# Which units read x's first two chunks from stepped copies, and where the copies are made, in a three-block transformer kernel on one core

## The chip, the core and the metric

The kernel runs on one core of one Trainium2 chip. The metric is the device time of one execution in microseconds. Times inside an execution are counted from the start of its span, the time between its first and its last instruction. TensorE is called PE, VectorE DVE, ScalarE ACT and GpSimd POOL in the rows of the profile.

## What is computed

For x of 256 tokens by 1024 features the kernel runs three blocks in turn, each a mixing layer and a feed-forward part:

```python
x = x + gla_layer_mix(rmsnorm(x, g_mix[0]), mem_k, mem_v, ...)   # block A: gated linear attention + memory attention
x = x + conv_ffn(rmsnorm(x, g_ffn[0]), w_up[0], ...)             # f0
shared = nsa_shared_kv(x, g_kv, w_kv, ...)                       # kv
x = x + nsa_layer_mix(rmsnorm(x, g_mix[1]), shared, ...)         # block B: sparse attention + memory attention
x = x + conv_ffn(rmsnorm(x, g_ffn[1]), w_up[1], ...)             # f1
x = rmsnorm(x, g_final)
h = concat([meta, x]); h = h + mix(rmsnorm(h, norm1_w))          # block C: forgetting attention + pooling
out = h + (silu(n2 @ w_gate) * (n2 @ w_up)) @ w_down             # f2, n2 = rmsnorm(h, norm2_w)
```

All of it is float32. Nearly all the work is in the products of normalized activations and weights.

## The kernel before

**Units.** The weights are cut into 146 units of 128 x 2048 columns, named in the order in which they are used (`Aq`, `Ak`, `Am0`, ..., `f0u0`, `f0u1`, ..., `f0d10`, `kvc`, `kvk`, `Bq0`, ...). SyncE loads a unit into one of three slots of `raw`; ScalarE casts it to a high part `wh` in the fp32r format, VectorE subtracts to get the low part `wl` (line 1279). Activations are split in the same way, in eight chunks of 128 features by 256 tokens: ScalarE writes the high part of a chunk with its gain, VectorE the low part (`enter`, line 1287), and `x_lo` counts the chunks entered. A product is then three matmuls: high by high, low by high and high by low (`mm3`), all issued at line 417. The division by the norm is done later, on the products.

**Forms of a unit on PE.** `unit_f` (line 435) and `part_f` (line 456, a range of chunks) keep a block of 128 columns of weights stationary and move a chunk of x through: for each chunk two blocks of three matmuls, so 48 matmuls for a unit and 6 for a chunk. `unit_t` (line 491) has x stationary and moves the weights, for two tiles of 128 tokens: 3 matmuls for a chunk and tile, so 48 for a unit as well. Each waits for the unit's low weights (`w_low`) and for each chunk (`ready(c)`). Every engine runs its own program in the order written, so that what stands behind a wait waits too.

**Where the operands lie.** Each chunk of x lies in `xh` and `xl` at a pitch of 320 columns, and its 256 tokens begin at column 48 modulo 64 of the partition, for every chunk. The memory and the attention's outputs lie in `coh` and `col` with the chunk offsets

```python
CO = [0, 256, 512, 768, 1568, 1840, 1024, 1280]
```

so that all chunks begin at 48 modulo 64 but chunk 4, at 16, and chunk 5, at 32. Weights begin at 0 modulo 64 (at 32 for the units of `unit_t`, at 48 for `Ck` and `Cu`).

**The copies.** `xkh` and `xkl` hold copies of chunks 0 and 1 of x at a pitch of 272 columns, so that they begin at 16 and at 32. POOL makes them (`first_two`, line 2532: four copies of 128x256, lines 2536 and 2537) once the low part of chunk 1 is there, and counts them in `x_two`. They are made for A, f0, f1, C and f2. They are called stepped copies here. With the argument `two`, `unit_f` reads chunks 0 and 1 from them, after a wait on `x_two`. Before the change these units do so: `Am1`; u2, u3 and u5 of each feed-forward part (`ffn`, line 633); u12 of f1; and `Cq1`.

**The order around the change.** u2 and u3 stand behind short breaks in the run of large matmuls: `sums` (four products of one column, for the variances) and `norm_spread` (two transposes). `Am0`'s first half stands behind `sums`, `Bq0` behind `norm_spread`, `m0k0` behind the products of `tri`, `Av0` and `Av1` behind small products of the memory attention, and the halves of `Bm0` and `Bm1` behind small products of the sparse and the memory attention. u5 stands behind `down(tag, 0)`, 48 large matmuls, and u12 of f1 behind the sums of the meta tokens. POOL also computes the powers for the norms (`power`, line 2527), in its program's order: ..., first_two f0, power f0, power B, two memsets, first_two f1, ...

Of the kernel before, what the change touches and what calls it, by code (L numbers as in the profile page):

```python
# [142 lines left out]
ENTER = {n: 8 * i for i, n in enumerate(["A", "mem0", "mem1", "f0", "kv", "B", "f1"])}  # L143
ENTER.update(meta=56, C=57, f2=65)
NORM = {n: i for i, n in enumerate(["A", "mem", "f0", "B", "f1", "f2"])}
TWO = {n: i for i, n in enumerate(["A", "f0", "f1", "C", "f2"])}
POW = {n: i for i, n in enumerate(["A", "mem", "gla", "f0", "B", "f1", "meta", "C1", "C2", "q", "k", "f2"])}

SQ = {"A": 0, "mem": 8, "f0": 16, "B": 24, "f1": 32, "meta": 40, "f2": 41}
RES = {"f0": 0, "f1": 4, "f2": 8}  # L150
POOLED = [0, 2, 5, 9]
MIX = {"f0": 0, "f1": 1, "f2": 2}
KORD = [0, 1, 2, 3, 4, 5, 6, 7]
KOUT = [4, 5, 6, 7, 0, 1, 2, 3]
NR = NH = 3
# [12 lines left out]
def program(nc, ctx, w_d, x_d, mem_d, meta_d, small_d, const_d, gmask_d, nsac_d, sel_d, out_d):  # L168
# [246 lines left out]
    def pe_program(pe, t):  # L415
# [16 lines left out]
            m = src.shape[0]  # L432
            return pe.transpose(out, src, cn("ident")[0:m, 0:m])  # L433

        def unit_f(name, bank, a_h, a_l, ready, two=None):


            i = U[name]
            H, L = v3(wslot(wh, i), 256), v3(wslot(wl, i), 256)
            P = ps.open(name, bank)  # L440
            t.wait_ge(*ps.vacant(name))
            for c in range(8):
                t.wait_ge(*w_low(i, c // 4))
                t.wait_ge(*ready(c))
                if two and c < 2:
                    t.wait_ge(*x_two.at(TWO[two]))
                    x_h, x_l = XKH(c), XKL(c)
                else:
                    x_h, x_l = a_h(c), a_l(c)
                for j in range(2):  # L450
                    o = slice(j * 128, (j + 1) * 128)
                    last = mm3(P[:, j * 256:j * 256 + T], H[:, c, o], L[:, c, o], x_h, x_l, c == 0 and j == 0, c == 7)
            last.then_inc(*ps.full(name))
            used[i] = ps.ready(name)

        def part_f(name, bank, chunks, ready, a_h=XH, a_l=XL):

            i = U[name]
            H, L = v3(wslot(wh, i), 256), v3(wslot(wl, i), 256)
            if chunks[0] == 0:  # L460
                ps.open(name, bank)
                t.wait_ge(*ps.vacant(name))
            P = ps[name]
            for c in chunks:
                t.wait_ge(*(w_lo0.at(QUART.index((i, c // 2))) if i < 2 else w_low(i, c // 4)))
                t.wait_ge(*ready(c))
                for j in range(2):
                    o = slice(j * 128, (j + 1) * 128)
                    last = mm3(P[:, j * 256:(j + 1) * 256], H[:, c, o], L[:, c, o], a_h(c), a_l(c), c == 0 and j == 0, c == 7)
            if chunks[-1] == 7:  # L470
                last.then_inc(*ps.full(name))
                used[i] = ps.ready(name)
# [15 lines left out]
            if 1 in blocks:  # L488
                used[i] = ps.ready(f"{name}.1")

        def unit_t(name, bank, a_h, a_l, ready, tiles=(0, 128), turn=(0, 1)):

            i = U[name]
            H, L = v3(wslot(wh, i), 256), v3(wslot(wl, i), 256)
            for n, a in enumerate(tiles):
                if n not in turn:
                    continue
                at = f"{name}.{n // 2}"
                if n % 2 == 0:
                    ps.open(at, bank())  # L500
                    t.wait_ge(*ps.vacant(at))
                O = ps[at][:, (n % 2) * 256:(n % 2) * 256 + 256]
                for c in range(8):
                    t.wait_ge(*w_low(i, c // 4))
                    t.wait_ge(*ready(c))
                    mm(O, a_h(c)[:, a:a + 128], H[:, c, :], c == 0, False)
                    mm(O, a_l(c)[:, a:a + 128], H[:, c, :], False, False)
                    last = mm(O, a_h(c)[:, a:a + 128], L[:, c, :], False, c == 7)
                if n % 2 == 1:
                    last.then_inc(*ps.full(at))  # L510
            if len(tiles) - 1 in turn:
                used[i] = ps.ready(at)
# [120 lines left out]
        def ffn(tag):  # L633
            x_in = entered(tag)
            unit_f(f"{tag}u0", bank_a(), XH, XL, x_in)
            unit_f(f"{tag}u1", bank_a(), XH, XL, x_in)
            sums(tag, bank_b())
            unit_f(f"{tag}u2", bank_a(), XH, XL, x_in, tag)
            norm_spread(tag, bank_b(), rst_)
            unit_f(f"{tag}u3", bank_a(), XH, XL, x_in, tag)  # L640
            unit_f(f"{tag}u4", bank_a(), XH, XL, x_in)
            down(tag, 0)
            unit_f(f"{tag}u5", bank_a(), XH, XL, x_in, tag)
            down(tag, 1)
            for p in range(2, 10):
                unit_f(f"{tag}u{2 * p + 2}", bank_a(), XH, XL, x_in, tag if tag == "f1" and p == 5 else None)
                unit_f(f"{tag}u{2 * p + 3}", bank_a(), XH, XL, x_in)
                down(tag, p)
                if tag == "f1" and p == 4:
                    meta_sums()  # L650
            down(tag, 10)
# [12 lines left out]
        quarters(P, T, lambda c: wn[:, c, :], lambda c: xs[c], True, True).then_inc(*ps.full("alr"))  # L664
        t.wait_ge(*d_cst.at(0))
        sums("A", bank_b())
        part_f("Am0", bank_a(), range(0, 4), x_a)
        norm_spread("A", bank_b(), rst_)
        part_f("Am0", None, range(4, 8), x_a)

# [71 lines left out]
        last.then_inc(*ps.full("tri"))  # L742
        m_0, m_1 = entered("mem0"), entered("mem1")
        qA = lambda h: f"Am{h // 2}"
        unit_f("m0k0", bank_a(), CH, CL, m_0)
        unit_f("m0k1", bank_a(), CH, CL, m_0)
        level(0)
        sums("mem", bank_b())
# [20 lines left out]
        mem_scores(0, 3, bank_b(), mqA, qA)  # L769
        mem_turn(0, 1, bank_b())  # L770
        mem_out(0, 0, bank_b())
        unit_t("Av0", bank_a, XH, XL, x_a)
        mem_turn(0, 2, bank_b())
        mem_out(0, 1, bank_b())
        unit_t("Av1", bank_a, XH, XL, x_a)
        mem_turn(0, 3, bank_b())
        mem_out(0, 2, bank_b())
        summed(0)
# [150 lines left out]
        sums("B", 4)  # L929
        part_f("kvk", 1, range(4, 8), kv_in, CH, CL)  # L930
        norm_spread("B", 5, rst_)
        unit_f("Bq0", 3, XH, XL, x_b)
        P = ps.open("gates", 0)
        t.wait_ge(*ps.vacant("gates"))
        t.wait_ge(*s_wn.at(1))
# [19 lines left out]
        squeeze(1, 0, 2)  # L955
        nsa_scores(2)
        squeeze(1, 1)
        part_f("Bm0", 1, range(0, 4), x_b)
        nsa_scores(3)
        P = ps.open("gT", 0)  # L960
        t.wait_ge(*ps.vacant("gT"))
# [20 lines left out]
        blocks_scores(1, None)  # L982
        nsa_out(2)
        mem_scores(1, 0, 4, mqB, qB)
        part_f("Bm1", 1, range(0, 4), x_b)
        nsa_turn(3)
        mem_scores(1, 1, 0, mqB, qB)
        part_f("Bm1", 1, range(4, 8), x_b)
# [1532 lines left out]
    def pool_program(g, q):  # L2521
        def power(tag, dst, src, ready):

            q.wait_ge(*ready)
            half = cn("mhalf")[0:src.shape[0], :]
            half = half.unsqueeze(2) if len(src.shape) == 3 else half
            g.tensor_tensor(dst, src, half.broadcast_to(list(src.shape)), ALU.pow).then_inc(*s_pow.up(POW[tag]))

        def token_power(tag, dst=rst_[:, 0:2]):
            power(tag, dst, rst_[:, 8:10], ps.done("sums_" + tag))  # L2530

        def first_two(tag):

            q.wait_ge(*x_lo.at(ENTER[tag] + 1))
            for c in range(2):
                g.tensor_copy(XKH(c), XH(c))
                last = g.tensor_copy(XKL(c), XL(c))
            last.then_inc(*x_two.up(TWO[tag]))

        g.memset(wn_[:, :], 0.0).then_inc(*s_wn0.up(0))  # L2540
        g.memset(AT_, 0.0).then_inc(*g_at0.up(0))  # L2541
        first_two("A")
        q.wait_ge(*d_cst.at(0))
        token_power("A")
        token_power("mem", mrst)
        power("gla", rr[:, 8:16], rr[:, 0:8], ps.done("sums_gla"))
        first_two("f0")
        token_power("f0")
        token_power("B")
        q.wait_ge(*ps.ready("cmp0"))  # L2550
        g.memset(pc_, 0.0)
        g.memset(vcm, 0.0).then_inc(*n_zero.up(0))
        first_two("f1")
        token_power("f1")
        power("meta", rst_[0:NM, 2:3], rst_[0:NM, 10:11], ps.done("sums_meta"))
        first_two("C")
        power("C1", r2[:, 6:8], r2[:, 0:2], c_var.at(0))
        power("C2", r2[:, 8:10], r2[:, 2:4], c_var.at(2))
        power("q", hr[:, 0:2, 0:8], v3(hv[:, 0:16], 8), ps.done("hsum_q"))
        power("k", hr[:, 2:5, 0:8], v3(hv[:, 16:40], 8), ps.done("hsum_k"))  # L2560

        k = 0
        for p in range(4):
            bufs = [pa, pb] if p % 2 == 0 else [sqh[:, 0:TM], sqh[:, TM:2 * TM]]
            src, n, lo = uu[:, p, :], 1, 0
            q.wait_ge(*ps.done(f"Cu{p // 2}.{p % 2}"))
            if p >= 2:
                q.wait_ge(*(p_out.at(p // 2 - 1) if p % 2 == 0 else ps.ready(f"po{p // 2 - 1}")))
            if p == 1:
                q.wait_ge(*ps.ready("hscale_q1"))  # L2570
            for i in range(p + 1):
                dst = bufs[i % 2]
                lo += n
                if i:
                    q.wait_ge(*p_sum.at(k - 1))
                g.tensor_tensor(dst[:, lo:TM], src[:, lo:TM], src[:, lo - n:TM - n], ALU.add).then_inc(*p_sum.up(k))
                src, n, k = dst, 2 * n, k + 1
        first_two("f2")
        token_power("f2")
# [214 lines left out]
```

## Time and profile before

| | |
|---|---|
| median of 3 runs | 896.84 us (896.43 to 896.90) |
| the profiled execution | 896.14 us |
| its span | 894.4 us |
| PE busy | 887.4 us (99%) |
| DVE busy | 648.5 us (73%) |
| ACT busy | 494.3 us (55%) |
| POOL busy | 43.1 us (5%) |
| DMA | 160.68 MB, mean 180 GB/s |
| granted clock | 1.00 |

Matmuls are pipelined: each of them is shown with some 280 ns, but the next begins after some 115 ns. So the busy time of PE says only that it is hardly ever idle. How fast it works is read from the times between the starts of matmuls, in its timeline: the start of a later one less the start of an earlier one, by the number of steps between them. Where a break stands before a unit, its first matmul is 200 to 300 ns ahead of its second, so that steps are counted from the second on.

### The profile page before, as it was taken

What the parts mean: (1) busy time and instruction counts of PE and PEld (TensorE: products, weight loads), DVE (VectorE), ACT (ScalarE), POOL (GpSimd) and SP (SyncE); (2) the same over time, 40 slices, a digit from 0 to 9 for tenths busy, and PEclk for the clock granted to TensorE, in tenths of its full rate; (3) what the DMA queues carried; (4) which work ended last, traced back from release to release, by engine and by line L of the source; (5) the groups of instructions that cost most, each with busy time, mean ns of one, the idle gap of its engine ahead of it and who ended that gap; (6) DMA issues with size and microseconds to landing.
All of it is one profiled execution on the core that took longest, in us unless ns stands there. A gap on an engine that the chain in (4) does not pass through costs nothing.

```text
span 894.4 us, 18695 instructions
## 1 busy us (share of the span) xinstructions
PE 887.4 (99%) x7883; PEld 861.5 (96%) x7883; DVE 648.5 (73%) x1191; ACT 494.3 (55%) x849; POOL 43.1 (5%) x50
## 2 busy tenths in 40 slices
PE   8999999999999999999999999999999999999998
PEld 7999999999999998889999999999988999999998
DVE  6987657877767789785887767678688586565664
ACT  6763555564545567575565546547447464444451
POOL 2000001000000000000100000001142000000000
DMA  8743343555465444633556654654162255546541
GB/s 318 291 178 111 137 154 137 229 224 208 144 233 189 171 162 163 241 125 99 214 184 236 211 198 170 219 206 138 52 237 95 95 220 207 195 181 212 201 154 48
DMA packets 26002, 160.68 MB, mean 180 GB/s; under 512 B 3008, under 2 KB 4928, under 8 KB 7360
## 3 DMA queue, kind: packets, MB, share of 16 engines
q1 hardware_dynamic: 25344, 158.45, 48.8%
q8 instruction: 62, 1.02, 0.5%
q10 hardware_dynamic: 576, 1.05, 0.4%
q14 instruction: 20, 0.16, 0.1%
HBM read 158.18 MB, written 1.05 MB: 178 GB/s over the span
## 4 chain that ended last, share of the span: by engine, by line
PE 95%; DVE 3%; DMA 1%; issue 0%; SPq 0%; ACT 0%
PE ps L417 94%; PE ps L433 2%; DVE wl L1279 1%; DMA raw<-in_w 1%; DVE arena L1729 0%; DVE arena L1970 0%; DVE arena L2002 0%; DVE arena L2014 0%; DVE arena L1966 0%; DVE arena L1713 0%; DVE arena L1976 0%; SPq L2584 0%; DVE arena L1785 0%; DVE arena L2003 0%; DVE arena L2025 0%
## 5 line engine op out<-in xcount | busy, mean ns | idle before, releaser
L1279 DVE TENSOR_TENSOR wl<-raw,wh 128x1024 fp32r<-128x1024 f32 x280 | 329.3, 1223 | 124.6 <-ACT wh L2077 124.2
L417 PE MATMUL ps<-xh,wh 128*128 128x256 f32 (+1 forms) x1264 | 352.3, 279 | 0.7 <-DVE wl L1495 0.7
L417 PE MATMUL ps<-xl,wh 128*128 128x256 f32 (+1 forms) x1264 | 350.1, 277 | 0.0
L417 PE MATMUL ps<-xh,wl 128*128 128x256 f32 (+1 forms) x1264 | 350.0, 277 | 0.0
L2077 ACT CAST wh<-raw 128x1024 fp32r<-128x1024 f32 x280 | 277.2, 1047 | 114.8 <-PE ps L417 105.0
L417 PEld LDWEIGHTS ps<-xh,wh 128*128 128x128 f32 x1264 | 237.5, 188 | 3.0 <-DVE wl L1495 1.5
L417 PEld LDWEIGHTS ps<-xl,wh 128*128 128x128 f32 x1264 | 237.4, 188 | 0.1
L417 PEld LDWEIGHTS ps<-xh,wl 128*128 128x128 f32 x1264 | 237.4, 188 | 0.0
L417 PE MATMUL ps<-fh,wl 128*128 128x256 f32 x528 | 145.8, 276 | 0.0
L417 PE MATMUL ps<-fh,wh 128*128 128x256 f32 x528 | 145.8, 276 | 0.0
L417 PE MATMUL ps<-fl,wh 128*128 128x256 f32 x528 | 145.8, 276 | 0.0
L417 PEld LDWEIGHTS ps<-fl,wh 128*128 128x128 f32 x528 | 99.1, 188 | 0.0
L417 PEld LDWEIGHTS ps<-fh,wh 128*128 128x128 f32 x528 | 99.1, 188 | 0.0
L417 PEld LDWEIGHTS ps<-fh,wl 128*128 128x128 f32 x528 | 99.1, 188 | 0.0
L417 PE MATMUL ps<-coh,wh 128*128 128x256 f32 x288 | 81.5, 283 | 0.5 <-DVE col L1988 0.5
L417 PE MATMUL ps<-col,wh 128*128 128x256 f32 x288 | 80.0, 278 | 0.0
L417 PE MATMUL ps<-coh,wl 128*128 128x256 f32 x288 | 79.9, 277 | 0.0
L2166 ACT ACTIVATE arena<-arena,small 128x256 f32<-128x256 f32 x44 | 22.4, 510 | 74.2 <-DVE arena L1409 74.2
L417 PEld LDWEIGHTS ps<-coh,wh 128*128 128x128 f32 x288 | 54.1, 188 | 1.2 <-issue 0.9
L417 PEld LDWEIGHTS ps<-col,wh 128*128 128x128 f32 x288 | 54.1, 188 | 0.1
L417 PEld LDWEIGHTS ps<-coh,wl 128*128 128x128 f32 x288 | 54.1, 188 | 0.0
L417 PE MATMUL ps<-arena 64*128 64x128 f32 (+7 forms) x342 | 35.5, 316 | 2.0 <-POOL arena L2541 2.0
(257 smaller groups left out, 1052.8 us busy)
## 6 DMA issues: line engine op xcount, KB each, us to landing
raw<-in_w SPq DMA_DIRECT2D x144, 1024.0 KB, 4.9
raw<-in_w ACTq DMA_DIRECT2D x4, 256.0 KB, 5.3
xt<-in_x SPq DMA_DIRECT2D x4, 256.0 KB, 6.6
raw<-in_w SPq DMA_DIRECT2D x4, 256.0 KB, 8.2
arena<-in_mem SPq DMA_DIRECT2D x1, 1024.0 KB, 8.5
out<-xt SPq DMA_DIRECT2D x8, 128.0 KB, 1.9
arena<-in_sel SPq DMA_DIRECT2D x3, 256.0 KB, 5.6
small<-in_small SPq DMA_DIRECT2D x1, 623.0 KB, 6.1
```

The source lines that it names most:

```text
L417: return pe.matmul(out, lhsT, rhs, start=start, stop=stop, skip_group_check=True)
L433: return pe.transpose(out, src, cn("ident")[0:m, 0:m])
L1279: v.tensor_tensor(L[:, s], src[:, s], f32(H[:, s]), ALU.subtract).then_inc(*w_lo.up(split(i, a)))
L2077: s.copy(H[:, cs], src[:, cs]).then_inc(*w_hi.up(split(i, n)))
L2166: s.activation(yb[f % 2][:, 0:T], ab[f % 2][:, 0:T], ACT.Copy, scale=sm(cw, f, f + 1)).then_inc(*f_y.up(k0 + f))
```

## The change

The copies are made for B too, behind its power on POOL. A table says for each of the six inputs which of chunks 0 and 1 are read from them. `part_f` and `unit_t` learn to read them, the latter in its first token tile alone. `unit_f` takes an order of chunks.

```diff
-TWO = {n: i for i, n in enumerate(["A", "f0", "f1", "C", "f2"])}
+TWO = {n: i for i, n in enumerate(["A", "f0", "B", "f1", "C", "f2"])}
+STEPPED = {"A": (0, 1), "f0": (0, 1), "B": (0, 1), "f1": (0,), "C": (0, 1), "f2": (1,)}
...
-        def unit_f(name, bank, a_h, a_l, ready, two=None):
+        def unit_f(name, bank, a_h, a_l, ready, two=None, order=KORD):
...
-            for c in range(8):
+            for c in order:
                 t.wait_ge(*w_low(i, c // 4))
                 t.wait_ge(*ready(c))
-                if two and c < 2:
+                if two and c in STEPPED[two]:
                     t.wait_ge(*x_two.at(TWO[two]))
                     x_h, x_l = XKH(c), XKL(c)
...
-        def part_f(name, bank, chunks, ready, a_h=XH, a_l=XL):
+        def part_f(name, bank, chunks, ready, a_h=XH, a_l=XL, two=None):
...
+                if two and c in STEPPED[two]:
+                    t.wait_ge(*x_two.at(TWO[two]))
+                    x_h, x_l = XKH(c), XKL(c)
+                else:
+                    x_h, x_l = a_h(c), a_l(c)
...
-        def unit_t(name, bank, a_h, a_l, ready, tiles=(0, 128), turn=(0, 1)):
+        def unit_t(name, bank, a_h, a_l, ready, tiles=(0, 128), turn=(0, 1), two=None):
...
+                    if two and n == 0 and c in STEPPED[two]:
+                        t.wait_ge(*x_two.at(TWO[two]))
+                        x_h, x_l = XKH(c)[:, a:a + 128], XKL(c)[:, a:a + 128]
...
-            unit_f(f"{tag}u5", bank_a(), XH, XL, x_in, tag)
+            unit_f(f"{tag}u5", bank_a(), XH, XL, x_in)
...
-        part_f("Am0", bank_a(), range(0, 4), x_a)
+        part_f("Am0", bank_a(), range(0, 4), x_a, two="A")
...
-        unit_f("m0k0", bank_a(), CH, CL, m_0)
+        unit_f("m0k0", bank_a(), CH, CL, m_0, order=KOUT)
...
-        unit_t("Av0", bank_a, XH, XL, x_a)
+        unit_t("Av0", bank_a, XH, XL, x_a, two="A")
...
-        unit_t("Av1", bank_a, XH, XL, x_a)
+        unit_t("Av1", bank_a, XH, XL, x_a, two="A")
...
-        unit_f("Bq0", 3, XH, XL, x_b)
+        unit_f("Bq0", 3, XH, XL, x_b, "B", (2, 3, 0, 1, 4, 5, 6, 7))
...
-        part_f("Bm0", 1, range(0, 4), x_b)
+        part_f("Bm0", 1, range(0, 4), x_b, two="B")
...
-        part_f("Bm1", 1, range(0, 4), x_b)
+        part_f("Bm1", 1, range(0, 4), x_b, two="B")
...
         token_power("B")
+        first_two("B")
         q.wait_ge(*ps.ready("cmp0"))
```

`KOUT` is 4, 5, 6, 7, 0, 1, 2, 3. In f1 the units u2, u3 and u12 now read chunk 0 from the copy and chunk 1 in place, in f2 the units u2 and u3 chunk 1 from the copy and chunk 0 in place. `Am1`, `Cq1` and f0's u2 and u3 are as before.

## Rows read from the trace of the kernel before

**Rows 1.** The head of the page and its first part (busy time, share, instructions).
```profile
span 894.4 us, 18695 instructions
PE 887.4 (99%) x7883; PEld 861.5 (96%) x7883; DVE 648.5 (73%) x1191; ACT 494.3 (55%) x849; POOL 43.1 (5%) x50
```

**Rows 2.** Page part 4, then the chain: start us, us, what.
```profile
PE 95%; DVE 3%; DMA 1%; issue 0%; SPq 0%; ACT 0%
...
728.23 163.35 PE ps L417 x1440
```

**Rows 3.** Timeline of PE, unit Bq0: start us, us, engine, line, operation, operands.
```profile
341.38 0.28 PE L417 MATMUL ps<-xl,wh 128*128 128x256 f32 x1
...
346.80 0.28 PE L417 MATMUL ps<-xh,wl 128*128 128x256 f32 x1
```

**Rows 4.** Timeline of PE, unit f0u2, second matmul, first on x itself, last.
```profile
160.64 0.28 PE L417 MATMUL ps<-xkl,wh 128*128 128x256 f32 x1
...
161.94 0.28 PE L417 MATMUL ps<-xh,wh 128*128 128x256 f32 x1
...
165.92 0.28 PE L417 MATMUL ps<-xh,wl 128*128 128x256 f32 x1
```

**Rows 5.** Timeline of PE, unit f0u5, first matmul and first on x itself.
```profile
182.65 0.28 PE L417 MATMUL ps<-xkh,wh 128*128 128x256 f32 x1
...
184.06 0.28 PE L417 MATMUL ps<-xh,wh 128*128 128x256 f32 x1
```

**Rows 6.** Timeline of PE, unit Av0, second and last matmul.
```profile
107.11 0.28 PE L417 MATMUL ps<-wh,xl 128*128 128x256 f32 x1
...
112.52 0.28 PE L417 MATMUL ps<-wl,xh 128*128 128x256 f32 x1
```

**Rows 7.** Timeline of PE, unit m1v1, its matmuls 2, 22 and 40.
```profile
99.35 0.28 PE L417 MATMUL ps<-wh,col 128*128 128x256 f32 x1
...
101.72 0.28 PE L417 MATMUL ps<-wh,coh 128*128 128x256 f32 x1
...
103.76 0.28 PE L417 MATMUL ps<-wh,coh 128*128 128x256 f32 x1
```

**Rows 8.** Timeline of PE, unit m0k0, its matmuls 2 and 47.
```profile
35.89 0.28 PE L417 MATMUL ps<-col,wh 128*128 128x256 f32 x1
...
41.17 0.28 PE L417 MATMUL ps<-col,wh 128*128 128x256 f32 x1
```

**Rows 9.** Timeline of PE, second half of kvk, second and last matmul.
```profile
338.37 0.28 PE L417 MATMUL ps<-col,wh 128*128 128x256 f32 x1
...
340.93 0.28 PE L417 MATMUL ps<-coh,wl 128*128 128x256 f32 x1
```

**Rows 10.** Timeline of PE, first half of Am0, second and last matmul.
```profile
21.55 0.28 PE L417 MATMUL ps<-xl,wh 128*128 128x256 f32 x1
...
24.14 0.28 PE L417 MATMUL ps<-xh,wl 128*128 128x256 f32 x1
```

**Rows 11.** Timeline of PE, first half of Bm0, second and last matmul.
```profile
374.94 0.29 PE L417 MATMUL ps<-xl,wh 128*128 128x256 f32 x1
...
377.45 0.28 PE L417 MATMUL ps<-xh,wl 128*128 128x256 f32 x1
```

**Rows 12.** Timeline of POOL, copies, power for B; in brackets idle before and releaser.
```profile
7.70 0.59 POOL L2537 CAST xkl<-xl 128x256 fp32r<-128x256 f32 x1
8.24 0.58 POOL L2536 CAST xkh<-xh 128x256 fp32r<-128x256 f32 x1
...
140.35 0.40 POOL L2536 CAST xkh<-xh 128x256 fp32r<-128x256 f32 x1 [9.32 <-DVE xl L1287]
...
141.04 1.39 POOL L2536 CAST xkh<-xh 128x256 fp32r<-128x256 f32 x1
...
339.64 0.86 POOL L2527 TENSOR_TENSOR rst<-rst,cst 128x2 f32<-128x2 f32 x1 [175.68 <-DVE rst L1304]
```

**Rows 13.** Timeline of DVE, low parts of the memory's chunks, then of B's.
```profile
33.09 3.25 DVE L1287 SCALAR_TENSOR_TENSOR col<-arena,small,coh 128x256 fp32r<-128x256 f32 x8
...
339.47 3.25 DVE L1287 SCALAR_TENSOR_TENSOR xl<-xt,small,xh 128x256 fp32r<-128x256 f32 x8
```

More of the change, by code:

```diff
@@ L451, in unit_f @@
                     o = slice(j * 128, (j + 1) * 128)
-                    last = mm3(P[:, j * 256:j * 256 + T], H[:, c, o], L[:, c, o], x_h, x_l, c == 0 and j == 0, c == 7)
+                    last = mm3(P[:, j * 256:j * 256 + T], H[:, c, o], L[:, c, o], x_h, x_l,
+                               c == order[0] and j == 0, c == order[-1])
             last.then_inc(*ps.full(name))
             used[i] = ps.ready(name)
-        def part_f(name, bank, chunks, ready, a_h=XH, a_l=XL):
+        def part_f(name, bank, chunks, ready, a_h=XH, a_l=XL, two=None):
             i = U[name]
@@ L466, in part_f @@
                 t.wait_ge(*ready(c))
+                if two and c in STEPPED[two]:
[3 more added lines that the diff above has]
+                    x_h, x_l = a_h(c), a_l(c)
                 for j in range(2):
                     o = slice(j * 128, (j + 1) * 128)
-                    last = mm3(P[:, j * 256:(j + 1) * 256], H[:, c, o], L[:, c, o], a_h(c), a_l(c), c == 0 and j == 0, c == 7)
+                    last = mm3(P[:, j * 256:(j + 1) * 256], H[:, c, o], L[:, c, o], x_h, x_l, c == 0 and j == 0, c == 7)
             if chunks[-1] == 7:
@@ L505, in unit_t @@
                     t.wait_ge(*ready(c))
-                    mm(O, a_h(c)[:, a:a + 128], H[:, c, :], c == 0, False)
-                    mm(O, a_l(c)[:, a:a + 128], H[:, c, :], False, False)
-                    last = mm(O, a_h(c)[:, a:a + 128], L[:, c, :], False, c == 7)
+                    if two and n == 0 and c in STEPPED[two]:
+                        t.wait_ge(*x_two.at(TWO[two]))
+                        x_h, x_l = XKH(c)[:, a:a + 128], XKL(c)[:, a:a + 128]
+                    else:
+                        x_h, x_l = a_h(c)[:, a:a + 128], a_l(c)[:, a:a + 128]
+                    mm(O, x_h, H[:, c, :], c == 0, False)
+                    mm(O, x_l, H[:, c, :], False, False)
+                    last = mm(O, x_h, L[:, c, :], False, c == 7)
                 if n % 2 == 1:
```

## The prediction

> **What bounds the kernel now.** I read the page's head and its first part, then the chain that ended last, then PE's timeline matmul by matmul. TensorE is busy for 99% of a span of 894.4 us [rows 1], PE is 95% of the chain that ended last, and that chain's last 163 us are one unbroken run of 1440 matmuls [rows 2]. So the question is what one matmul costs, start to start. All of these matmuls have the same shape (128x256), and the granted clock is 1.00 throughout, the 2.4 GHz level. Yet two paces show. The run of 1440 takes 163.35 / 1440 = 113.4 ns each [rows 2]. Unit Bq0, behind two transposes, starts its second matmul at 341.38 and its last, 46 further on, at 346.80: 117.8 ns each [rows 3]. I call these the short pace (113.33 ns) and the long pace (117.8 ns); the difference is 4.5 ns a matmul.
>
> What switches between them can be read from the operands. f0u2, behind a break too, reads the copies first: 11 steps from 160.64 to 161.94 are 118.2 ns each, at the long pace, but the 35 steps from there to 165.92, on x itself, are 113.7 ns [rows 4]. Its excess over the short pace is (165.92 - 160.64) - 46 x 0.11333 = 0.067 us; that of Bq0, which reads x alone, is 5.42 - 5.213 = 0.207 us [rows 3]. A break (transposes, sums, small matmuls) can leave PE at the long pace, it stays there as long as every chunk of x begins at the same place modulo 64 columns (48 by the layout), and it ends on the return from the copies, whose chunks begin at 16 and 32. The copies themselves always run long: f0u5, in the middle of a short stretch with no break before it, goes from 182.65 to 184.06 over its 12 copied matmuls, 117.5 ns each [rows 5]. So a copy pays after a break that left PE long, and costs elsewhere.
>
> **The change part by part.** PE has next to no slack, so each saved step counts in full unless said. Excesses are over the short pace.
>
> (1) The fifth up unit of the three feed-forward parts (u5) loses its copies. There is no break before it: 12 steps at 117.5 become 113.3 [rows 5], 0.05 us, and the first steps after the return cost 0.01 more. Three units of this kind: -0.18 us.
>
> (2) Av0 and Av1 read copies for chunks 0 and 1 of their first token tile. Here x is the stationary operand. Av0 runs long from 107.11 to 112.52, 46 steps of 117.6 [rows 6], an excess of 0.20 us, and Av1, the same unit on other weights, is taken alike. The nearest unit with a stationary operand that steps in the same way is m1v1, whose chunks 4 and 5 begin at 16 and 32: long to 101.72, then 18 steps to 103.76 at 113.3, and long again after the next such passage [rows 7]. With x stationary the passage toggles the pace. Only one passage is in each unit and both begin long, so about 6 + 3 matmuls stay long: 0.20 - 0.05 = 0.15 us each, -0.30 us. If the copied start comes out short, the toggle makes the rest long and the gain is nothing: bounds 0 and -0.35.
>
> (3) m0k0 reads chunks 4 to 7 first. Now it is long until chunk 6: 45 steps from 35.89 to 41.17, an excess of 5.28 - 5.10 = 0.18 us [rows 8]. The second half of kvk begins behind a break on chunk 4 and takes 2.56 us for 22 steps [rows 9], an excess of 0.067. So -0.11 us. Chunk 4 of the memory, needed at 35.7, is the fifth of eight VectorE operations that fill 33.09 to 36.34, ready by about 35.15 [rows 13]: no new wait, and its price if that cover were gone is the 0.4 us of one such operation.
>
> (4) Am0's first half runs long: 22 steps from 21.55 to 24.14, an excess of 0.10 [rows 10], and becomes 0.067: -0.03 us. The copies for A are made before 10 us (the second of the four begins at 7.70 [rows 12]).
>
> (5) Bq0 reads chunks 2, 3, 0, 1, 4 to 7 with copies for 0 and 1. The first 24 matmuls stay long, the last 24 get short: 0.207 becomes 0.12, -0.085 us. But the copies for B are new work on GpSimd and a new wait on PE, with everything behind it in PE's queue. GpSimd runs its power for B from 339.64 to 340.50 [rows 12] and can copy only then. PE needs the copies at the 13th matmul of Bq0, 341.38 + 11 x 0.118 = 342.68 [rows 3]. In those microseconds VectorE is at its eight operations on the same chunks, 339.47 to 342.72 [rows 13]. A copy beside such operations of VectorE took 0.59 us (at 7.70), with the next 0.54 us later (8.24); alone it took 0.40 us, beside the long weight subtractions 1.39 us [rows 12]. So four copies end at 340.55 + 3 x 0.54 + 0.59 = 342.8 by the nearest row, 342.0 by the shortest and about 346.0 by the longest. With the hand-over PE then stalls for 0.25 us (bounds 0 and 3.4). VectorE's own operations grow by some tenths there, hidden under its wait for Bq0's end.
>
> The trace shows the two lengths of the copy beside VectorE's work [rows 12, 13]. The Trainium skill, GPSIMD Engine Reference, section "Specifications", says that GpSimd shares its SBUF interfaces with VectorE and contends with VectorE instructions that have two SBUF inputs. By it the copies would be slowed for as long as those operations run; without it they would end 0.8 us sooner and the stall would be gone.
>
> (6) The first halves of Bm0 and Bm1 read copies. Bm0's is short by itself: 22 steps from 374.94 to 377.45 are 2.51 us, an excess of 0.02 [rows 11]. With copies it has the 0.067: +0.05 us, a loss. Bm1's is the same but ends in a stretch where PE waits for VectorE a few microseconds later, so I cost it at nothing; without that cover +0.05.
>
> (7) In f1, u2, u3 and u12 copy chunk 0 alone, in f2 u2 and u3 copy chunk 1 alone. If the return from one copy still ends the long pace, 6 fewer copied matmuls at 4.5 ns are 0.03 us each: f1 -0.09; in f2 the chunk now read in place comes first behind the break and may be long anyway, -0.03. Neither step (16 to 48, or 48 to 32 to 48) occurs in this trace.
>
> Sum: -0.18 - 0.30 - 0.11 - 0.03 - 0.085 + 0.25 + 0.05 - 0.09 - 0.03 = about -0.53 us. Against its own time the profiled execution of before (896.14 us, span 894.4) would come to 895.6; it lies 0.7 us under the median of the three runs, 896.84, from which I forecast **896.3 us**.
>
> **The rivals.**
> The single copy fails. If a step of one chunk doesn't end the long pace, it isn't a matter of one unit: no break follows f2u3, and 1440 matmuls [rows 2] at 4.5 ns more are +6.4 us, 902.7 in all. In f1 the long pace would last from u3 to the meta tokens' sums and from u12 to the end, by the program's order 672 and some 800 matmuls, +6.6 us, about 902.9; both, 909. For it: with x stationary the passage toggled the pace instead of setting it [rows 7], and chunk 1 alone, read after a chunk in place, would toggle a short start to long. Against it: wherever x or the memory is the moving operand, the step from 32 back to 48 ended in the short pace [rows 4, 8, 9], and f2 keeps that step. It decides from a long pace that survives chunk 2 of u3.
>
> The wait at Bq0 becomes the bound. If VectorE's weight subtractions meet the copies, each takes 1.39 us [rows 12], PE stalls for 3.4 us instead of 0.25 and the kernel is slower: 896.3 + 3.1 = 899.4. It is slower than before from a stall of 0.8 us on. Against it: those subtractions begin only when the eight operations have ended [rows 13].
>
> The stationary copies don't switch the pace (Av0, Av1 as before): 896.6. The stall is nil and Bm0's copies cost nothing: 896.0. Both lie within 0.2% of before.
>
> The edit doesn't touch the pace at all, since a matmul's cost would depend on its size alone. Then only the wait stays: 896.84 + 0.25 = 897.1. Against it stand the two paces of one shape [rows 2, 3] and f0u5, where only the operand's place differs [rows 5]. The Trainium skill, TensorE: Matmul & The Clock Gate, section "Back-to-back issue gap", gives such a rule, a gap of N/2.4 + 2.5 ns for an isolated matmul of N columns, whatever its operands' places; the trace disagrees with it, at 113.3 and 117.8 ns.
>
> **How the numbers follow.** The sum above holds with a chance of 0.78 (0.12 of that for its variants at 896.6 and 896.0), a failing single copy has 0.10, the wait at Bq0 as bound 0.06, the pace untouched 0.02; 0.04 is for gains beyond my sum, if the remaining long stretches (Bq1, Bm0 and Bm1's second halves, some 0.1 us each) and others change over too. The bounds of the terms give 895.4 to 897.2; the runs of before differ by 0.5 us, and a stall of up to 1.5 us belongs in: 895.2 to 897.9. A measurement of this kernel can tell about 0.2%, 1.8 us, from no change. Every case of the sum lies within that; faster by more has 0.04, slower by more the two rivals, with a part of the second that stays under it: 0.13.
>
> **What would show it.** In the profile after: f0u5, f1u5, f2u5 without copies at 113.3 ns a step; Av0 and Av1 short from their third chunk on, 0.15 us shorter each; m0k0 short from its 16th matmul; four new copies on GpSimd from about 340.5, of 0.5 to 0.6 us, and a gap in Bq0 before its 13th matmul; Bm0's first half 0.05 us longer. Wrong would be: f1 or f2 at 117.8 ns through their long runs, copies of 1.4 us at 341, or a gap in Bq0 beyond 1 us.

## The result: 3.5 us slower, and where they are

| | before | after |
|---|---|---|
| median | 896.84 us (3 runs), 896.84 (5 runs of the same session as after) | 900.33 us (5 runs, 899.90 to 900.83) |
| profiled execution, its span | 896.14, 894.4 us | 900.83, 899.2 us |
| granted clock | 1.00 | 1.00 |

The ratio is 1.004, with a 95% interval of 1.003 to 1.0051. The forecast was 896.3 with a range up to 897.9, so it was wrong. The interval lies wholly above 1: the kernel is slower by some 0.4%.

The head of after's page, to be read against [rows 1] (start with the span and PE's busy time):

```profile
span 899.2 us, 18699 instructions
PE 891.5 (99%) x7883; PEld 865.8 (96%) x7883; DVE 649.2 (72%) x1191; ACT 494.8 (55%) x849; POOL 45.6 (5%) x54
```

PE has the same 7883 matmuls and is again busy for 99%. Four instructions are new on POOL. So the loss is either in the pace or in short waits, and the page shows neither. The timeline does. First f1 from u12 on (start us, us, engine, line, operation, operands): before, then after, from u12's second matmul through the rest of f1 to the last one of `Cq0`, the first unit of block C, which follows f1 without a break.

```profile
524.81 0.28 PE L417 MATMUL ps<-xkl,wh 128*128 128x256 f32 x1
...
617.13 0.28 PE L417 MATMUL ps<-xh,wl 128*128 128x256 f32 x1
```

```profile
525.52 0.28 PE L418 MATMUL ps<-xkl,wh 128*128 128x256 f32 x1
...
526.11 0.28 PE L418 MATMUL ps<-xh,wh 128*128 128x256 f32 x1
...
530.93 0.28 PE L418 MATMUL ps<-xh,wl 128*128 128x256 f32 x1
...
621.39 0.28 PE L418 MATMUL ps<-xh,wl 128*128 128x256 f32 x1
```

By the program these are 814 steps. Before they take 92.32 us, 113.4 ns each; after 95.87 us, 117.8 ns each: **+3.55 us**. Nothing waits there; each matmul begins 4.4 ns later than before. u12 itself shows where it starts: from its return to x itself at 526.11 its last 41 steps to 530.93 are 117.6 ns each. The single copy of chunk 0 did not end the long pace, and no break follows until Cq0 has ended.

f2 is another matter: the chain ends with one run, as before [rows 2], now at 113.4 ns (start, us, what).

```profile
733.09 163.29 PE ps L418 x1440
```

So chunk 1 alone works there. The other parts, in the order of the forecast, are in these lines of after: the second and last matmul of each stretch (u5 of f0: its first and thirteenth).

```profile
182.86 0.28 PE L418 MATMUL ps<-xh,wh 128*128 128x256 f32 x1
...
184.22 0.28 PE L418 MATMUL ps<-xh,wh 128*128 128x256 f32 x1
```

```profile
107.50 0.28 PE L418 MATMUL ps<-wh,xkl 128*128 128x256 f32 x1
...
112.74 0.28 PE L418 MATMUL ps<-wl,xh 128*128 128x256 f32 x1
...
114.28 0.28 PE L418 MATMUL ps<-wh,xkl 128*128 128x256 f32 x1
...
119.70 0.28 PE L418 MATMUL ps<-wl,xh 128*128 128x256 f32 x1
```

```profile
21.96 0.28 PE L418 MATMUL ps<-xkl,wh 128*128 128x256 f32 x1
...
24.54 0.28 PE L418 MATMUL ps<-xh,wl 128*128 128x256 f32 x1
...
25.00 0.28 PE L418 MATMUL ps<-xl,wh 128*128 128x256 f32 x1
...
27.59 0.28 PE L418 MATMUL ps<-xh,wl 128*128 128x256 f32 x1
```

- u5 takes 1.36 us for 12 steps, 113.3 ns each, where it was 1.41 [rows 5].
- Av0 takes 5.24 us where it took 5.41 [rows 6]. Av1 takes 5.42 us for its 46 steps, as in the kernel before: no gain.
- m0k0, from 36.40 to 41.56, takes 5.16 us where it was 5.28 [rows 8].
- Am0's first half takes 2.58 us instead of 2.59 [rows 10], but its **second** half, whose code was not touched, takes 2.59 us (25.00 to 27.59). Before it was 2.51, from 24.60 to 27.11. So the pace has turned over at the break between the halves. But this is only in part the edit's: in the profiled executions of b_f0_zero, b_f0_zero_tr and g_u5_u12, which leave Am0 as it was, the halves took 2.50 and 2.59 us.

Around Bq0, POOL first, then DVE, then PE:

```profile
340.61 0.54 POOL L2548 CAST xkh<-xh 128x256 fp32r<-128x256 f32 x1
341.10 0.59 POOL L2549 CAST xkl<-xl 128x256 fp32r<-128x256 f32 x1
341.64 0.58 POOL L2548 CAST xkh<-xh 128x256 fp32r<-128x256 f32 x1
342.17 0.59 POOL L2549 CAST xkl<-xl 128x256 fp32r<-128x256 f32 x1
```

```profile
339.62 3.81 DVE L1299 SCALAR_TENSOR_TENSOR xl<-xt,small,xh 128x256 fp32r<-128x256 f32 x8
...
347.81 0.87 DVE L1705 SCALAR_TENSOR_TENSOR memkv<-ps,arena,rs 128x256 f32<-128x256 f32 x2
```

```profile
341.54 0.28 PE L418 MATMUL ps<-xl,wh 128*128 128x256 f32 x1
...
342.84 0.36 PE L418 MATMUL ps<-xkh,wh 128*128 128x256 f32 x1
343.04 0.28 PE L418 MATMUL ps<-xkl,wh 128*128 128x256 f32 x1
...
346.96 0.28 PE L418 MATMUL ps<-xh,wl 128*128 128x256 f32 x1
347.16 1.07 PE L418 MATMUL ps<-xt,wn 128*32 128x256 f32 x16
348.54 1.58 PE L418 MATMUL ps<-arena,memkv 64*128 64x128 f32 x16 [0.30 <-DVE memkv L1705]
```

The copies are as long as forecast and end at 342.76; the step behind PE's 13th matmul, the first on a copy, is 0.20 us instead of 0.12, as behind a break. So the wait costs 0.08 us, the later short pace gives it back, and Bq0 takes 5.42 us, as in [rows 3]. But DVE's eight operations on B's chunks take 3.81 us instead of 3.25 [rows 13]. At 341.54 PE is 0.16 us later than before (341.38), but everything behind those operations in DVE's queue is 0.69 us later, down to the two operations at line 1705 (1693 before) for which PE waits (347.81 against 347.12). The same two places of PE before:

```profile
347.01 1.07 PE L417 MATMUL ps<-xt,wn 128*32 128x256 f32 x16
348.01 1.58 PE L417 MATMUL ps<-arena,memkv 64*128 64x128 f32 x16
```

From the gates' products to the next, 1.00 us has become 1.38: **+0.38 us**.

The profiled execution is 4.8 us of span longer, the medians differ by 3.5. The rest is one execution's own: after reaches Am0 0.4 us later (its second matmul at 21.96 against 21.55), and its wait for DVE at line 2000 near 686 us was 1.0 us, where before and two experiments with the same code there had 0.5. Of the 0.4 us, 0.24 are the pace again: the 58 steps ahead of Am0, which no run's edit touches, took 6.59 us in before and 6.83 in after. Of the 14 profiled executions in this document five took 6.58 or 6.59 and nine 6.83, kernels with the same code there on both sides. So the pace there differs from one profiled execution to another though the code is the same, and f1's doesn't follow from it.

### The profile page after: what moved, and what is told of

Read it like the earlier page. It is cut to its first block, busy times and chain, and to the rows that moved or that the text cites. A ratio compares the mean times of both kernels' runs of the same rounds, so it can differ in the third digit from the quotient of the medians.

```text
span 899.2 us, 18699 instructions
## 1 busy us (share of the span) xinstructions
PE 891.5 (99%) x7883; PEld 865.8 (96%) x7883; DVE 649.2 (72%) x1191; ACT 494.8 (55%) x849; POOL 45.6 (5%) x54
## 4 chain that ended last, share of the span: by engine, by line
PE 92%; DVE 6%; DMA 1%; ACT 1%; issue 0%; SPq 0%
PE ps L418 90%; DVE wl L1291 2%; PE ps L434 2%; DMA raw<-in_w 1%; DVE arena L1741 0%; DVE xl L1299 0%; ACT coh L2101 0%; ACT wh L2089 0%; DVE xt L1487 0%; DVE arena L1982 0%; DVE col L1299 0%; DVE arena L2014 0%; DVE arena L2026 0%; DVE arena L1978 0%; ACT arena L2109 0%
```

## The experiments

In all of them the kernel before was run beside, with medians between 896.47 and 896.83.

**1 and 2. f1 with both copies, or with the other one.** The first edit is below; the second has `(1,)` in its place.

```diff
-STEPPED = {"A": (0, 1), "f0": (0, 1), "B": (0, 1), "f1": (0,), "C": (0, 1), "f2": (1,)}
+STEPPED = {"A": (0, 1), "f0": (0, 1), "B": (0, 1), "f1": (0, 1), "C": (0, 1), "f2": (1,)}
```

> The changed kernel with both copies in f1 again. Theory P (the single copy of chunk 0 leaves f1 at the long pace from u12 on): 3.4 to 3.6 us come back, about 896.8 to 897.0, and f1 from u12 to its end runs at 113.3 ns a matmul. Rival W (the wait and the copies for B are what costs): it stays above 899.5.

> The changed kernel with chunk 1 as f1's single copy. If the return from 32 to 48 ends the long pace whatever stood before it, u2, u3 and u12 get short after chunk 1 as in f2, and the time is that of both copies within 0.1 us, about 896.8. If the pace is set by the position of chunk 0 behind a break, u12 stays long: about 900.3.

Measured: 896.69 us (ratio 0.9999, 0.999 to 1.0009) and 896.77 us (1.0002, 0.9992 to 1.0011). The whole loss is in f1's table entry, and it is not that one copy is too few: chunk 1 alone is enough in u2, u3 and u12. In u12 it is the way from 16 straight to 48 that fails.

**3. One edit in the kernel before: u12 alone.**

```diff
-                if two and c < 2:
+                if two and c in ((0,) if name == "f1u12" else (0, 1)):
```

> The kernel before, with chunk 0 as the only copy in u12 of f1. Theory P: this one edit costs 3.4 us (some 760 matmuls at 4.5 ns), about 900.2. Rival (the long pace of u12 needs the other edits, which shift where everything starts): no change, 896.8.

Measured: 900.58 us, ratio 1.0044 (1.0028 to 1.0061). This one edit costs as much as the whole change. The single copies of f1u2 and f1u3 have no part in it.

**4. The same in f0's u2 and u3.**

```diff
+                if two and c in ((0,) if name in ("f0u2", "f0u3") else (0, 1)):
```

> The kernel before, with chunk 0 as the only copy in u2 and u3 of f0. Theory K (what counts is the kind of break: behind column products the single copy fails, behind transposes it works): u2 stays long to its end, +0.15 us, u3 gets short, about 897.0. Theory S (what counts is the slot of the unit's weights; in f1 the failing u2 and u12 lie in slot 0, the working u3 in slot 1): u2 of f0 lies in slot 1 and works; u3 lies in slot 2, which no unit of f1 shows: if it fails, all of f0 stays long, some 1440 matmuls, +6.4 us, about 903.2; if it works, 896.7.

Measured: 896.49 us, ratio 0.9999 (0.9989 to 1.0008). u2 and u3 behave differently. Second matmul, return to x and last matmul of u2; then the first two on x and the later one of u3:

```profile
161.26 0.28 PE L417 MATMUL ps<-xkl,wh 128*128 128x256 f32 x1
...
161.85 0.28 PE L417 MATMUL ps<-xh,wh 128*128 128x256 f32 x1
...
166.68 0.28 PE L417 MATMUL ps<-xh,wl 128*128 128x256 f32 x1
...
167.72 0.28 PE L417 MATMUL ps<-xh,wh 128*128 128x256 f32 x1
167.84 0.28 PE L417 MATMUL ps<-xl,wh 128*128 128x256 f32 x1
...
171.92 0.28 PE L417 MATMUL ps<-xl,wh 128*128 128x256 f32 x1
```

u2's 41 steps from 161.85 to 166.68 are 117.8 ns each, long to the end. u3's 36 from 167.84 to 171.92 are 113.3 ns: its single copy worked. The same pair is in after's f1 (u2 5.42 us from its second to its last matmul, u3 5.24 us). So the single copy fails behind one break and works behind another, and the weights' slot of a unit is not what decides: slot 1 holds f0u2, which failed, and f1u3, which worked.

This run shows one thing more. Bq0, whose code is the same as before, is short in it, from its second to its last matmul:

```profile
342.11 0.28 PE L417 MATMUL ps<-xl,wh 128*128 128x256 f32 x1
...
347.34 0.28 PE L417 MATMUL ps<-xh,wl 128*128 128x256 f32 x1
```

It takes 5.23 us instead of 5.42 [rows 3], and so again in experiment 5, which also has the single copies in f0; in the eight other kernels that read Bq0 in place and in the old order it took 5.42. Yet the code from f0u4 on is that of before, and PE ran it at the same paces up to the transposes ahead of Bq0 (the second half of kvk takes 2.56 us in both). Something from f0u2 or f0u3 reached Bq0, some 170 us later, that the pace just ahead of its break does not show.

**5. Is it the kind of break?** u3 stands behind two transposes, u2 and u12 behind sums. Here two transposes are put behind f0's sums too.

```diff
+            if tag == "f0":
+                for n in range(2):
+                    last = tr(P[:, 256 + n * 128:384 + n * 128], cn("inv", 0, 1).broadcast_to([128, 128]))
```

> The kernel before, chunk 0 as the only copy in u2 and u3 of f0, and two more transposes (of a constant) behind f0's column sums, straight before u2. Theory K (the kind of break before the unit decides): u2 now gets short after its sixth matmul as u3 does, its first 118 ns pitch is 117 to 118 instead of 121; the transposes themselves cost about 0.22 us. Rival (something else in u2, such as its weights or the sums' place): u2 stays at 117.7 ns to its end as without the transposes.

Measured: 896.96 us, ratio 1.0002 (0.9993 to 1.0011), and u2 stayed at 117.8 ns to its end. This theory (K in the expectations) fell.

**6. Is it the pace ahead of the break?** (Theory M; theory L says that the unit's place decides.) In every unit so far the single copy of chunk 0 failed where PE had run short ahead of the break and worked where it had run long. Here f1u2 keeps both copies, so that f1u3 stands behind a short u2. The run also gives Av1 its copies behind an Av0 in place.

```diff
+                if two and c in ((0,) if name in ("f1u3", "f1u12") else (0, 1)):
...
-        unit_t("Av1", bank_a, XH, XL, x_a)
+        unit_t("Av1", bank_a, XH, XL, x_a, two="A")
```

> The kernel before with chunk 0 alone copied in f1u3 and f1u12 (f1u2 keeps both), and with both chunks of Av1's first token tile read from copies while Av0 reads x in place. In the units seen so far a single copy failed where PE ran short ahead of the break (f0u2, f1u2, f1u12) and worked where it ran long ahead of it (f0u3 and f1u3, behind a u2 that had stayed long); Av1's copies failed behind a short Av0. Theory M (the pace ahead of the break decides): here f1u3 stands behind a short u2, so it fails and some 670 matmuls up to the meta tokens' sums run at 117.8 ns, +3.0 us; f1u12 then stands behind a long stretch, so its single copy works and the rest of f1 is at 113.3 ns; Av1 stands behind a long Av0, so it is short behind its copies, -0.17 us. About 899.5. Theory L (the unit's place decides): f1u3 works, f1u12 stays long to the end of f1, +3.5 us, and Av1 stays at 117.8 ns: about 900.3. If neither the place nor the pace ahead decides, other patterns (both fail: 903.2; both work: 896.6).

Measured: 901.0 us, ratio 1.005 (1.0034 to 1.0065): neither of the two sums. f1u3, which had worked in after, now failed. But the long pace did not last to the meta tokens' sums: the copies of f1u5, which the kernel before has, ended it at about 467 us, so it cost 0.6 us instead of 3.0. That had been overlooked. So f1u12 stood behind a short stretch again and failed, +3.55 us, which both theories then say. These two make 4.1 of the 4.5 us between the medians. Av1 stayed long, against theory M.

**7. The same with f1u5 in place,** so that f1u12 does stand behind a long stretch.

```diff
+                if two and c in ((0,) if name in ("f1u3", "f1u12") else () if name == "f1u5" else (0, 1)):
```

> The kernel before with chunk 0 alone copied in f1u3 and f1u12, both chunks in f1u2, and f1u5 in place, so that nothing ends a long pace between f1u3 and the meta tokens' sums (in the run e_mirror the copies of f1u5 ended it). Theory M (a single copy ends the long pace only where PE ran long ahead of the break): f1u3 fails behind a short f1u2 and the 670 matmuls up to the meta tokens' sums run at 117.8 ns, +3.0 us; f1u12 then stands behind a long stretch, works, and the rest of f1 is at 113.3 ns: 899.5 to 899.8. Theory L (the place of f1u12 decides): it fails behind a long stretch too, and the whole of f1 from f1u3 on is long: 3.0 + 3.5 = 6.5 us more, about 903.1.

Measured: 899.58 us, ratio 1.003 (1.0019 to 1.0041), as theory M had it; theory L had 903.1. f1u3 from its second matmul to its last, the end of the long stretch, then u12:

```profile
448.85 0.28 PE L417 MATMUL ps<-xkl,wh 128*128 128x256 f32 x1
...
454.26 0.28 PE L417 MATMUL ps<-xh,wl 128*128 128x256 f32 x1
...
527.75 0.28 PE L417 MATMUL ps<-fh,wl 128*128 128x256 f32 x1
...
528.67 0.28 PE L417 MATMUL ps<-xkl,wh 128*128 128x256 f32 x1
...
533.92 0.28 PE L417 MATMUL ps<-xh,wl 128*128 128x256 f32 x1
```

u3 takes 5.41 us, u12 5.25 us (5.41 in after), with the same instructions on the same operands as in after. Just ahead of the break the two traces differ in PE's pace alone: 117.8 ns here, 113.3 in after. f1u3 is the same comparison the other way round: behind a u2 that had stayed long it took 5.24 us (after), behind a short u2 5.41 (e_mirror and this run). That the pace itself decides, and not something that goes along with it, is not shown; Bq0 in experiment 4 speaks for more than the pace.

**8. A single copy without a break, in f0u5.**

```diff
+                if two and c in ((0,) if name == "f0u5" else (0, 1)):
```

> The kernel before with chunk 0 alone copied in f0u5, which has no break before it and stands in a short stretch. If a single copy behind a short stretch turns PE long whether or not a break stands between (theory M without the break), all matmuls from f0u5 to the sums for B, some 1360, run at 117.8 ns: +6.1 us, about 902.7, with f0u5's pitches at 118 after the copy. If it takes the break as well (theory M with the break), the six copied matmuls cost 0.03 us and the pace returns to 113.3 ns: 896.6.

Measured: 896.56 us, ratio 0.9997 (0.9988 to 1.0007). The six copied matmuls run at 118 ns, the third step behind them is at 114 again. So in this unit, with no break ahead of it, a single copy did not cost the short pace.

**9. What the part for B costs.** First the changed kernel with both copies in f1 and nothing for B; then the kernel before with B's copies made and read by nobody.

```diff
-        first_two("B")                                       # c_nob; Bq0, Bm0, Bm1 as before
```

```diff
         token_power("B")
+        first_two("B")                                       # b_bcopies
```

> The changed kernel with both copies in f1 and everything for B taken out: no copies made for B, Bq0, Bm0 and Bm1 read x in place in the old order. What is left gains by the PE starts of the run before it (both copies in f1): A's part 0.26 us, the three u5 0.18. Theory D (the copies for B slow VectorE's eight operations, so that the queries after Bq0 come 0.37 us late): about 896.6 - 0.45 = 896.2, and the pitch behind the gates' products is 309 ns again instead of some 680. Rival (the 0.37 us come from elsewhere): 896.6.

> The kernel before with the four copies for B made behind the power for B and read by nobody. Theory D: VectorE's eight operations on B's chunks take about 3.8 us instead of 3.25, the queries come late, PE loses about 0.45 us behind the gates' products: about 897.05. Rival (the reads at Bq0 and its wait are what costs): no change.

Measured: 896.06 us, ratio 0.9992 (0.9983 to 1.0001), and 897.04 us, ratio 1.0003 (0.9994 to 1.0012). The times can't tell 0.4 us, the traces can. With copies that nobody reads:

```profile
339.89 3.81 DVE L1287 SCALAR_TENSOR_TENSOR xl<-xt,small,xh 128x256 fp32r<-128x256 f32 x8
```

```profile
347.42 1.07 PE L417 MATMUL ps<-xt,wn 128*32 128x256 f32 x16
348.80 1.58 PE L417 MATMUL ps<-arena,memkv 64*128 64x128 f32 x16 [0.31 <-DVE memkv L1693]
```

1.38 us from the gates' products to the next, as in after. So POOL's copies slow DVE, and DVE holds PE; neither the wait in Bq0 nor its order does it.

**10. The cover put back.** a_f1_one, with half of DVE's weight subtractions for kvv moved behind its operations for the queries:

```diff
-        rests("kvk", 2)
+        rest("kvv", halves=(0,))
         take("spread_B", rs_[:, 0:T], T)
...
         queries(0)
+        rest("kvv", halves=(1,))
```

> The changed kernel with chunk 1 as f1's copy, and on VectorE the second half of kvv's weights subtracted behind the first queries instead of before them. Theory D: the 0.37 us behind the gates' products go, the copies for B cost only the wait in Bq0 (0.1), and the time is about 896.3. Rival: the wait moves to kvv's weights, 896.7.

Measured: 896.19 us, ratio 0.9993 (0.9984 to 1.0002). DVE's eight operations still take 3.81 us, but PE no longer waits:

```profile
347.29 1.07 PE L418 MATMUL ps<-xt,wn 128*32 128x256 f32 x16
348.29 1.58 PE L418 MATMUL ps<-arena,memkv 64*128 64x128 f32 x16
```

**11. Only what paid:** u5 and Av1 in place, Av0 with its copies, m0k0 from chunk 4 on, both copies in f1, nothing for B and Am0.

> The changed kernel with only what paid: u5 in place (-0.18 us), Av0 copied and Av1 in place (-0.17), m0k0 beginning with chunk 4 (-0.11), f1 with both copies, f2 as changed; Am0 as before and nothing for B. By the sum of the parts that the traces showed 896.8 - 0.46 = 896.3 to 896.4, no 0.37 us step at the gates. If the parts were not additive, or the steps of the f1 and B parts cost something in themselves, it would stay at 896.8 or above.

Measured: 896.08 us, ratio 0.9996 (0.9987 to 1.0004), beside 896.47 for before. The interval holds 1, so it isn't shown to beat the kernel before, though the parts that the earlier traces showed add up to -0.46 us. One thing came unasked: Av1, in place behind a short Av0, was short by itself, its second and last matmul at

```profile
114.12 0.28 PE L418 MATMUL ps<-wh,xl 128*128 128x256 f32 x1
...
119.34 0.28 PE L418 MATMUL ps<-wl,xh 128*128 128x256 f32 x1
```

5.22 us where it is 5.42 in the kernel before (114.06 to 119.48), behind a long Av0.

## Why the prediction was wrong, step by step

**The premise held.** Two paces of one matmul, 113.3 and 117.8 ns, that last until something changes them, show in all runs. The rival of a pace untouched fell. But the operands' places do not settle the pace: Bq0 and the steps ahead of Am0 ran at either one with the same instructions. And the formula that the prediction takes from the Trainium skill, TensorE: Matmul & The Clock Gate, section "Back-to-back issue gap", is for an isolated matmul; no run here measures one, so the back-to-back paces don't contradict it.

**Step (7) failed, and it decided the sign.** It put -0.09 us on f1's single copy and gave its failure 0.10. The mechanism of that rival was right and its term for u12 too (some 800 matmuls at 4.5 ns, 3.6 us; measured 3.55), but its place was not: u3's copy worked, so nothing was lost between u3 and the meta tokens' sums, and f2 kept its pace. The argument against the rival was that the step from 32 back to 48 always ended in the short pace. That holds in every unit with x as the moving operand and explains f2. It says nothing of f1, whose step is from 16 to 48, as the prediction itself noted ("Neither step ... occurs in this trace"). A step that had never been seen, with 3.6 us behind it, was priced at its good end: against 0.09 us to gain, that was the item to give the weight. f2's own -0.03 us was nothing: f2u2 and f2u3 take 5.29 us from their second to their last matmul, where they took 5.28, since chunk 0 in place is long behind the break.

**What the runs put in its place.** With chunk 0 alone copied behind a break, the pace behind a break was the reverse of the pace ahead of it: short ahead, long behind in f0u2 (twice), f1u2, f1u12 (three kernels) and f1u3 (two kernels); long ahead, short behind in f0u3 (twice), f1u3 in after, and f1u12 in g_u5_u12. Two units, f1u12 and f1u3, were seen both ways on the same instructions, and the outcome changed with the pace ahead. Why PE keeps such a thing across a break, no run shows. It isn't the whole rule either: Av1 with copies stayed long behind a short and behind a long Av0, and Bq0 in the two kernels of experiments 4 and 5 changed its pace though the pace ahead was the same. A hidden state that a break or a single copy turns over, and that the pace ahead mostly gives away, would fit too; nothing here separates the two.

**Step (5): the wait was mis-sized, its cover was wrong.** POOL's copies took 0.54 to 0.59 us, as forecast, and the wait was 0.08 instead of 0.25 us, since the copies ended at 342.76 and PE was 0.16 us late itself. The failed sentence is that VectorE's growth was "hidden under its wait for Bq0's end". There was no such slack: before, DVE's two operations at line 1693 ran from 347.12 to 348.00, and PE's products with their result began at 348.01. The growth of 0.56 us came out on PE as 0.38 (experiment 9). The Trainium skill, GPSIMD Engine Reference, section "Specifications", says that GpSimd shares its SBUF interfaces with VectorE and contends with VectorE instructions that have two SBUF inputs; the prediction used that for the copies alone. The trace agrees, and for both sides: the copies took 0.54 to 0.59 us against 0.40 alone, VectorE's operations 3.81 against 3.25.

**Step (2): half right.** Av0 gave 0.17 us instead of 0.15, short right from its return; Av1 gave nothing. The price was one passage taken from m1v1 for both; that Av1 would stand behind an Av0 that had become short was not weighed, and experiment 11 shows that in place it would then have been short anyway, 5.22 us against 5.42 with its copies.

**Step (4) missed the break behind it.** Between the two profiles Am0's first half gave 0.01 us (2.59 to 2.58) and its second half lost 0.08. All five kernels with copies in the first half had the second half at 2.59 us, but so had five of the nine without. The two halves together took 5.14 to 5.18 us with copies; without, 5.09 to 5.11 us in eight kernels and 5.18 in the ninth. So the copies gained nothing there and may have cost some hundredths. As with f_best's Av1, a unit that the edit left alone changed its pace where the one ahead of it had changed.

**As forecast:** u5, -0.05 to -0.06 each (step 1); m0k0, -0.12 (step 3); Bm0's first half, from 375.42 to 377.99 after, 2.57 us where it was 2.51 [rows 11], +0.06 (step 6).

**Step (6) had a cover that wasn't there.** Bm1's first half, which it costed at nothing, took 2.57 us (390.27 to 392.84) where it was 2.51 (389.72 to 392.23), and what follows kept its distance: the second matmul of Bm1's second half began 2.41 us behind it (2.40 before), and the next large matmuls 7.94 us behind Bm1's end (7.93). So the +0.06 came through. It may be one execution's own, since three kernels that read Bm1 in place had 2.59 there.

The sum from the trace: +3.55 (u12) + 0.14 (f1u2, 5.42 for 5.28) - 0.04 (f1u3, 5.24 for 5.28) + 0.38 (gates) + 0.07 (Am0) + 0.06 (Bm0) + 0.06 (Bm1) - 0.16 (u5, three) - 0.17 (Av0) - 0.12 (m0k0) = +3.8 us, beside +3.5 between the medians.

## What to carry to other kernels

Where a matmul has two paces and a small device ends the slow one, look first at how many matmuls stand behind each place of the device until the next break: here six copied matmuls guarded 814. An untried form of it is worth at most what it saves itself and can cost that whole stretch, so try it where a break follows soon. And new work on POOL beside DVE's operations lengthens these as well: follow DVE's queue to the first operation for which PE has no slack.

## What the runs showed of the hardware that was not expected

- The pace of back-to-back 128x256 matmuls at the granted clock 1.00 depends on what ran before a break. One unit, f1u12, with the same instructions and operands, took 5.25 us for 46 steps where PE had come to the break of 16 matmuls of one column at 117.8 ns, and 5.41 where it had come at 113.3. Bq0 took 5.23 or 5.42 us after a difference some 170 us earlier.
- It can differ with the code the same: 58 steps ahead of Am0 that no edit touches took 6.58 to 6.59 us in five profiled executions and 6.83 in nine.
- Chunks that begin at 32 modulo 64 ended the long pace on the return to 48 in every feed-forward unit that read them (u2 and u3 of f0, f1 and f2; f1u12); a chunk at 16 alone did so, behind a break, in the four cases with a long stretch ahead of the break and in none of the eight with a short one.
- A short pace survives six or twelve matmuls at the other place when no break stands ahead of them (f0u5).
- Four copies of 128x256 on POOL made eight DVE operations of the same size take 3.81 us instead of 3.25, in every kernel that had them.
